# Last four value rows gathered into free u slots, weights released later, VectorE and TensorE trading four rows

## The reference

```
q = (xb @ w_q).reshape(n, PEER_HEADS, 2, PEER_HALF)
s = jnp.einsum('nhpc,pkc->nhpk', q, sk)
sv, si = lax.top_k(s, PEER_TOPK)
cand = sv[:, :, 0, :, None] + sv[:, :, 1, None, :]
cand_id = si[:, :, 0, :, None] * PEER_KEYS + si[:, :, 1, None, :]
fv, fi = lax.top_k(cand.reshape(n, PEER_HEADS, PEER_TOPK * PEER_TOPK), PEER_TOPK)
eid = jnp.take_along_axis(cand_id.reshape(n, PEER_HEADS, PEER_TOPK * PEER_TOPK), fi, axis=-1)
gw = jax.nn.softmax(fv, axis=-1)
u = u_tab[eid]
act = jax.nn.gelu(jnp.einsum('nhkd,nd->nhk', u, xb), approximate=False)
return jnp.einsum('nhk,nhkd->nd', gw * act, v_tab[eid])     # then x = layer_norm(DN_ALPHA * x + y, ...)
```

## Time and profile before

| | us |
|---|---|
| median of three runs (lowest to highest) | 2753.99 (2752.51 to 2756.5) |
| profiled execution | 2754.48 |
| its span | 2752.7 |
| TensorE busy | 2439.5 (89%) |
| VectorE busy | 1649.9 (60%) |
| GpSimd busy | 1115.2 (41%) |
| ScalarE busy | 894.8 (33%) |

### The profile page before, as it was taken

How to read it: one execution, slowest core, us unless ns; L and a number is a source line. 1 busy time by engine, 2 the same in 40 slices (tenths; PEclk the granted TensorE clock), 3 DMA queues, 4 the chain that set the end, 5 groups by cost and what they waited for, 6 DMA issues and landing times.

```text
span 2752.7 us, 26590 instructions
## 1 busy us (share of the span) xinstructions
PE 2439.5 (89%) x8980; PEld 1563.1 (57%) x8980; DVE 1649.9 (60%) x3321; ACT 894.8 (33%) x1753; POOL 1115.2 (41%) x1239
## 2 busy tenths in 40 slices
PE   8998988777778978897787788999999999999999
PEld 6865543222224645452233235887878878886787
DVE  1257667767664367576776756546765555557553
ACT  1122121221211412222112214445854444446543
POOL 0016677777774036677777772004600000035000
PEclk9999999999999999999999999999999999999999
DMA  7359999999999479999999997546045555542553
GB/s 235 123 166 394 402 409 409 409 409 403 409 409 349 136 251 396 401 409 409 409 407 402 409 409 269 184 171 173 17 158 171 196 171 178 182 153 83 162 183 123
DMA packets 321132, 766.68 MB, mean 279 GB/s; under 512 B 22997, under 2 KB 171429, under 8 KB 320997
## 3 DMA queue, kind: packets, MB, share of 16 engines
q0 software_dynamic: 150208, 546.77, 50.3%
q1 hardware_dynamic: 169536, 217.69, 24.2%
q10 hardware_dynamic: 1252, 0.50, 0.1%
HBM read 763.83 MB, written 1.05 MB: 278 GB/s over the span
## 4 chain that ended last, share of the span: by engine, by line
PE 52%; DMA 19%; DVE 15%; POOL 6%; issue 5%; ACT 2%; ACTq 0%; DVEq 0%; POOLq 0%
PE ps L303 31%; PE acc L303 20%; DMA arena<-in_peer_u,arena 14%; POOL arena L1380 6%; DMA arena<-in_peer_v,arena 6%; DVE arena L1303 4%; DVE arena L1232 1%; DVE arena L1238 1%; DVE arena L1234 1%; DVE arena L1236 1%; DVE arena L1230 1%; PE ps L1742 1%; PE ps L1629 1%; DVE arena L1266 0%; DVE arena L1270 0%
## 5 line engine op out<-in xcount | busy, mean ns | idle before, releaser
L303 PE MATMUL acc<-arena 128*128 128x512 f32 (+2 forms) x2174 | 1011.9, 609 | 235.8 <-DMA arena<-in_peer_v,arena 132.8
L303 PEld LDWEIGHTS acc<-arena 128*128 128x128 f32 x2174 | 406.5, 200 | 820.4 <-issue 647.7
L1380 POOL DMA_INDIRECT arena<-in_peer_u,arena x512 | 485.2, 948 | 353.9 <-DVE arena L1276 162.3
L1380 POOL DMA_INDIRECT arena<-in_peer_v,arena x512 | 488.7, 954 | 176.4 <-issue 130.7
L1303 DVE CUSTOM_DVE_ANT_0 arena<-arena,ps 128x1024 f32<-128x1024 f32 x256 | 306.3, 1219 | 215.3 <-DMA arena<-in_peer_u,arena 213.2
L1303 DVE CUSTOM_DVE_ANT_0 arena<-arena,acc 128x1024 f32<-128x1024 f32 x256 | 305.7, 1219 | 176.0 <-DMA arena<-in_peer_u,arena 174.2
L333 DVE TENSOR_TENSOR lo_ring<-ring,hi_ring 128x2048 fp32r<-128x2048 f32 x136 | 310.3, 2291 | 167.9 <-ACT hi_ring L325 164.1
L303 PE MATMUL ps<-x_fm,ring 128*128 128x256 f32 (+2 forms) x1728 | 339.0, 358 | 12.7 <-DMA ring<-in_rglru_w_in 4.3
L303 PEld LDWEIGHTS ps<-x_fm,ring 128*128 128x128 f32 (+1 forms) x1728 | 297.1, 194 | 60.2 <-issue 11.5
L303 PE MATMUL ps<-hi_ring,x_hi 128*128 128x512 f32 x704 | 287.9, 409 | 9.5 <-DVE k_mem L1851 5.9
L325 ACT CAST hi_ring<-ring 128x2048 fp32r<-128x2048 f32 x136 | 258.2, 1912 | 72.2 <-DMA ring<-in_ffn_w 72.1
(11 more groups left out here) (390 smaller groups left out, 2313.8 us busy)
## 6 DMA issues: line engine op xcount, KB each, us to landing
ring<-in_ffn_w SPq DMA_DIRECT2D x132, 1024.0 KB, 5.5
ring<-in_peer_w_q SPq DMA_DIRECT2D x16, 1024.0 KB, 6.1
ring<-in_mlstm_w_in SPq DMA_DIRECT2D x12, 1024.0 KB, 5.3
ring<-in_w_out SPq DMA_DIRECT2D x8, 1024.0 KB, 5.0
arena<-in_peer_u,arena POOLq DMA_INDIRECT x512, 10.5
arena<-in_peer_v,arena POOLq DMA_INDIRECT x512, 10.9
ring<-in_cv_w_in SPq DMA_DIRECT2D x8, 1024.0 KB, 6.6
ring<-in_rglru_w_in SPq DMA_DIRECT2D x7, 1024.0 KB, 10.7
```

What stands on the lines that cost most here:

```text
L303: return pe.matmul(o, l, r, start=first, stop=last)
L1380: pool.indirect_dma_start(ring_[:, g % slots, :], None, table, bass.IndirectOffsetOnAxis(ix[j % 4][:, k:k + 1].bitcast(U32), 0), element_o ...
```

## The change

Value rows 12 to 15 of each stage no longer go into v slots 4 to 7. They go into u slots 0 to 3, which u rows 8 to 11 of group 15 have left, and have four semaphores of their own (`v_late0` to `v_late3`). Their gathers therefore wait for VectorE's use of these u rows and not for TensorE's use of value rows 4 to 7. The order of the gathers stays. At the start of stage 1 the first four u gathers wait in addition for the use of those four value rows of stage 0.

Of group 15 VectorE now adds value rows 8 to 11, and TensorE rows 0 to 7 and 12 to 15. Both numbers are four, as before. ScalarE makes the diagonal matrices of rows 12 to 15 in place of those of rows 8 to 11.

The weights held back wait for the use of value row 8, which is VectorE's, in place of value row 5, which was TensorE's.

The first excerpt is TensorE at the end of the first stage, before: value row 7 and rows 8 to 11, two products each, then the products of token tile 0 with `r.x0`. `v_rows` is the landing of a row in a v slot, `act_steps` here the diagonal matrix.

The last four gathers wait for VectorE's steps, where all nine waited for TensorE's. The diff:

```diff
...
+V_LATE = 4
...
                  + [f"u_rows{i}" for i in range(U_SLOTS)] + [f"v_rows{i}" for i in range(V_SLOTS)]
+                 + [f"v_late{i}" for i in range(V_LATE)]
                  + ["s5_b", "s5_c", "gate_blocks"])
...
                 if name in HELD:
-                    nc.sync.wait_ge(pe_steps, count_of(f"v used {HELD[name]}"))
+                    nc.sync.wait_ge(*by(f"v used {HELD[name]}"))
...
-        HELD = {"r.x0": TT * PR_HEADS * PR_K - 11, "w1.00.1": 2 * TT * PR_HEADS * PR_K - 11}
+        HELD = {"r.x0": TT * PR_HEADS * PR_K - 8, "w1.00.1": 2 * TT * PR_HEADS * PR_K - 8}
...
         NJ = TT * PR_HEADS
-        DVE_FROM = 12
+        DVE_ROWS = range(8, 12)
+        STAGE_ROWS = NJ * PR_K
+
+        def v_place(g):
+
+            i, at = divmod(g, STAGE_ROWS)
+            late = at - (STAGE_ROWS - V_LATE)
+            if late >= 0:
+                return u_ring[:, late, :], f"v_late{late}", 16 * (i + 1)
+            slot = g % V_SLOTS
+            earlier = g // V_SLOTS - (i if slot >= V_SLOTS - V_LATE else 0)
+            return v_ring[:, slot, :], f"v_rows{slot}", 16 * (earlier + 1)
         def on_dve(j, k):
-            return j == NJ - 1 and k >= DVE_FROM
+            return j == NJ - 1 and k in DVE_ROWS
...
                     g = PR_K * (NJ * i + j) + k
                     pe.wait_ge(act_steps, count_of(f"diag {i}.{j}.{k}"))
-                    pe.wait_ge(sems[f"v_rows{g % V_SLOTS}"], 16 * (g // V_SLOTS + 1))
+                    v_row, v_sem, v_count = v_place(g)
+                    pe.wait_ge(sems[v_sem], v_count)
                     for half in range(2):
-                        ins = mm(acc[:, 2 * t + half, :], diag[:, k, :], v_ring[:, g % V_SLOTS, 512 * half:512 * half + 512],
-                                 j % PR_HEADS == 0 and k == 0, (j, k) in ((PR_HEADS - 1, PR_K - 1), (NJ - 1, DVE_FROM - 1)))
+                        ins = mm(acc[:, 2 * t + half, :], diag[:, k, :], v_row[:, 512 * half:512 * half + 512],
+                                 j % PR_HEADS == 0 and k == 0, (j, k) in ((PR_HEADS - 1, PR_K - 1), (NJ - 1, PR_K - 1)))
                     ins.then_inc(pe_steps, TE.step(f"v used {g}"))
                     found[f"v summed {i}.{t}"] = (TE.who, TE.n)
...
                     if on_dve(j, k):
                     if j:
-                        act.wait_ge(pe_steps, count_of(f"v used {PR_K * (NJ * i + j - 1) + k}"))
+                        act.wait_ge(*by(f"v used {PR_K * (NJ * i + j - 1) + k}"))
                     act.activation(diag[:, k, :], ident[:, :], ACT.Copy, scale=coef[b][:, k:k + 1]).then_inc(act_steps, AC.step(f"diag {i}.{j}.{k}"))
...
             j = NJ - 1
-            for k in range(DVE_FROM, PR_K):
+            for k in DVE_ROWS:
                 g = PR_K * (NJ * i + j) + k
-                dve.wait_ge(sems[f"v_rows{g % V_SLOTS}"], 16 * (g // V_SLOTS + 1))
-                dve.scalar_tensor_tensor(x_tok[:, 1, :], v_ring[:, g % V_SLOTS, :], coef[j % 2][:, k:k + 1], x_tok[:, 1, :],
+                v_row, v_sem, v_count = v_place(g)
+                dve.wait_ge(sems[v_sem], v_count)
+                dve.scalar_tensor_tensor(x_tok[:, 1, :], v_row, coef[j % 2][:, k:k + 1], x_tok[:, 1, :],
                                          ALU.mult, ALU.add).then_inc(dve_steps, VE.step(f"v used {g}"))
                 dve.wait_ge(dve_steps, VE.n)
...
         def pool_peer(i):
-            def gather(j, k, ring_, sem_, slots, used, table):
+            def gather(j, k, row, sem_, label, table):
+                pool.indirect_dma_start(row, None, table,
+                                                  bass.IndirectOffsetOnAxis(ix[j % 4][:, k:k + 1].bitcast(U32), 0),
+                                                  element_offset=0).then_inc(sems[sem_], landed(sem_, label))
+
+            def gather_u(j, k):
                 g = PR_K * (NJ * i + j) + k
-                if g >= slots:
-                    pool.wait_ge(*by(f"{used} used {g - slots}"))
-                pool.indirect_dma_start(ring_[:, g % slots, :], None, table,
-                                                  bass.IndirectOffsetOnAxis(ix[j % 4][:, k:k + 1].bitcast(U32), 0),
-                                                  element_offset=0).then_inc(sems[f"{sem_}{g % slots}"], landed(f"{sem_}{g % slots}", f"{sem_} {g}"))
+                if i and g - STAGE_ROWS * i < V_LATE:
+                    pool.wait_ge(*by(f"v used {g - V_LATE}"))
+                if g >= U_SLOTS:
+                    pool.wait_ge(*by(f"u used {g - U_SLOTS}"))
+                gather(j, k, u_ring[:, g % U_SLOTS, :], f"u_rows{g % U_SLOTS}", f"u_rows {g}", u_table)
+
+            def gather_v(j, k):
+                g = PR_K * (NJ * i + j) + k
+                row, sem_, _ = v_place(g)
+                if on_late_slot(j, k):
+                    pool.wait_ge(*by(f"u used {g - (PR_K - V_LATE) + U_SLOTS}"))
+                elif g >= V_SLOTS:
+                    pool.wait_ge(*by(f"v used {g - V_SLOTS}"))
+                gather(j, k, row, sem_, f"v_rows {g}", v_table)
+
+            def on_late_slot(j, k):
+                return j == NJ - 1 and k >= PR_K - V_LATE
...
                     pool.wait_ge(dve_steps, count_of(f"ix {i}.{j}"))
                 for k in range(PR_K):
                     if j < NJ:
-                        gather(j, k, u_ring, "u_rows", U_SLOTS, "u", u_table)
+                        gather_u(j, k)
                     for v in values(j, k):
-                        gather(v // PR_K, v % PR_K, v_ring, "v_rows", V_SLOTS, "v", v_table)
+                        gather_v(v // PR_K, v % PR_K)
```

## The result

The changed kernel takes 2756.81 us (median of 20 runs, 2751.06 to 2762.51) against 2753.15 us of the kernel before in the same series (20 runs, 2748.40 to 2756.52): ratio 1.0014, 95% interval 1.0008 to 1.0020. That is +3.7 us, 0.14% slower, and the interval excludes 1; +2.6 us was forecast. The profiled execution took 2759.18 us, with a span of 2757.4 us and a mean granted clock of 0.968.

The account below looks back on a forecast made before the run. In the first tail row 15's landing ends last, TensorE 0.78 us behind; after the change TensorE, at half clock, ends the stage. Tails of +1.5 and +1.1 sum to +2.6 us on 2753.99: 2756.6 us, range 2752 to 2761.5 (8 in 10).

Parts of the forecast that it names:

- Landings: Both tails: with weights released later, rows land 1.28 us apart for longer; first tail's row 15 comes 1.9 us earlier.
- the fourth rival: Both tails: rows land no earlier, row 15 at 876.05 as today; same time as forecast, chance inside the forecast's 0.62.
- The first fall: Both tails: after a 4.4 us TensorE gap ahead of row 12 the clock halves; sum with `acc` 1.5 us later.
- The 5.5 us: Last four value rows on TensorE: time at half clock after the restart, adding 2.7 us to the rows.
- The 0.4 us back: Second tail: transposes at full clock, 1.09 us not 1.97; half the difference returns before ScalarE's first read, leaving +1.1.
- The weights: Held weights issued later: `r.x0` at 878 to 879 costs nothing in the first tail; second tail's weights arrive in time.
- the bound of 880.8: First tail: latest time at which `r.x0` can land for TensorE without costing anything.
- The third rival: First tail: `r.x0` lands late at 881.5, clock falls, transposes 3.4 us later; 2760.0 us in all, chance 0.08.
- thirteen microseconds of cover: Second tail: held weights there at 1686.3, thirteen microseconds before the unit that needs them at 1699.79.
- The second fall: Rival: clock falls again ahead of first tail's transposes and second tail's unit, 1.7 us each; 2760.0 us, chance 0.18.
- What is lost stays lost: First tail: the chain stays on TensorE for 35.29 us from 884.89, so any gain or loss before then remains.
- The first rival: Both tails: clock stays at 1.00 across the last rows, -0.8 and -1.7 us, sum -2.5; 2751.5 us, chance 0.12.

Follow-up runs that it names:

- fourth experiment: Changed kernel with 36 small matmuls filling TensorE's gap ahead of value row 12 in each stage's last group: 2753.82 us, ratio 1.0001 (0.9992 to 1.0010).

## Why the prediction was right, and where it was not

**Landings: right.** Row 12 at +6.40 and +6.31 us for the forecast +6.40; `r.x0` issued at +2.58 for +2.56; VectorE's adds done at +6.5 for +6.5. The late weights alone brought the rows forward too, the slots alone did not, so the price was put on the right cause, and the fourth rival falls. When row 15 lands is seen where VectorE adds it, with the weights alone: at +10.64 and +11.54, where +11.50 was forecast.

**The first fall: right in kind, in size for one tail.** The gaps were 4.46 and 4.35 us (4.4 forecast). In the first tail the clock stayed at 0.50 for 5.5 us after the restart (867.62 to 873.13), the very number taken, and the sum with `acc` came 1.6 us later (1.5 forecast). In the second it stayed for 2.8 us only (1675.85 to 1678.68), and the sum came 0.1 later, not 1.5. The 5.5 us, taken from two restarts that happened to agree, is not a constant of these tails.

**The 0.4 us back: wrong.** The transposes of the second tail did run at full clock, 1.09 us, but ScalarE was still casting weights (1687.59 to 1691.27) and its first read of them had to wait. It was so before: the cast (1685.36 to 1689.04) ended just as the first read began, at 1689.02. With the gaps of the kernel before filled, the unit came only 0.06 us earlier: the low clock had been hidden there by ScalarE.

**The weights: right.** TensorE went from the rows to `r.x0` without a wait at 877.30 (+16.1), inside the bound of 880.8 (+18.2); it took its half in 3.73 us for 3.7, and the transposes came at +21.97 for +21.9. The third rival falls, though with no margin to spare: once the clock stays up, `r.x0` is what ends the wait (2.22 us in the fourth experiment). In the second tail the prediction counts thirteen microseconds of cover, up to the unit. That was misread: ScalarE casts these weights first, from 1687.59 on (1685.36 before), some 14 us ahead of the unit, so there was next to no cover. It cost nothing in the changed kernel, whose cast follows VectorE's norm without a wait; with the first gap filled the second of the two casts waits 0.34 us for the weights, on the chain.

**The second fall: the rival that came.** It had its places and their gaps right (a gap of 1.9 us ahead of the first tail's transposes, 2.15 measured; one of up to 3.6 ahead of the second tail's unit, 2.45 measured), a chance of 0.18, and a price of 1.7 a tail that fits the second (1.5) and not the first, where the low stretch was 6.8 us long (2.8). Its sign, a gap of some 2 us, does not decide: with the trade alone the 2.15 us ahead of the transposes were followed by no fall. The tails of the profiled execution add up to the rival's +6.0 us, and the fall ahead of the unit came in all five profiles that have its gap; the one ahead of the transposes came in one of two. In what share of the 20 runs they come, and so how much of the +3.7 us they are, is not shown.

**What is lost stays lost: in the main.** Of the 4.4 us of the first tail 3.5 were left at the second. The rows read here do not show where the rest was made up.

**The first rival, made true.** With all gaps filled the clock stays at 1.00, and the time is 2751.01 us; the rival's price was 2751.5. Its terms were -0.8 and -1.7 us, the profile has -1.1 and -0.6. So the rival was near in size, and it was its condition that the changed kernel did not meet.

So the mechanism is the forecast one, TensorE's clock after a gap that the trade opens: the trade alone costs more, and with the first gap filled the rows run at 1.00 and a loss is no longer shown. That the time was met so closely is luck in part. The forecast stood on a median of 2753.99 us of three runs where the 20 have 2753.15, so 2756.81 is near to 2756.6 while the difference is +3.7 and not +2.6. And the difference itself has two errors that work against each other: the first falls are about 0.9 too large for these profiles (1.7 and not 2.6, with the 0.4 that did not come back), and the second falls, put at nothing in the sum, came.

## What to carry to other kernels

A trade that takes work from an engine on the path can open an idle gap ahead of what is left there; price the gap by the clock behind it, and then look for the next gap, since an engine that catches up waits again. Filling one gap can move the fall to the next, where it may cost more: fill them from the first one to the end of the path, or leave the one that is hidden. A clock that stays up and rows that land sooner were each worth nothing by themselves here and something together, so test the pairs, with the control that has only one of the two.

## What was not expected of the hardware

- Ahead of the first tail's transposes a gap of 2.15 us of TensorE was followed by a granted clock of 0.50 in the changed kernel, and a gap of 2.15 us at the same place was not with the trade alone; nor was one of 2.22 us just before (fourth experiment). The length of such a gap does not tell.
- Low stretches behind like gaps were 3.4, 6.8 or 10.2 us long (1702.57 to 1705.98, 883.37 to 890.20, 881.23 to 891.47 where the kernel before had two gaps filled); what a fall costs is a spread and not a number. The 20 runs of the changed kernel spread over 11.5 us, those of the kernel before over 8.1; what of this is the tails is not shown.
- Weights that load beside gathered rows slow the rows, from 1.28 us apart to about 1.75. The weights are slow too: where TensorE waited for `r.x0`, it was 16.3 us from issue to use before (859.51 to 875.80), 13.0 with the later gaps filled (864.92 to 877.96) and 11.9 with the weights alone (867.28 to 879.18), the fewer rows beside them the less.
